# Retrieval and recurrent mixer of a two-layer hybrid trunk as one unrolled program on one Trainium2 core

## The chip, the core and the metric

The kernel runs on one core of a Trainium2 chip. The core has five engines, each with its own instruction stream: TensorE (PE; its weight loads are shown as PEld), VectorE (DVE), ScalarE (ACT), GpSimd (POOL) and SyncE (SP), and 16 DMA engines that carry data between HBM and the on-chip memory. Engines meet only at semaphores. The metric is the device time of one launch, in microseconds (us).

## What is computed

Two streams run through the same two layers: the **sample** (512 latent tokens, in four tiles of 128) and the **prompt** (128 context tokens, one tile). D_MODEL is 1024, everything is float32. Each layer is a mixer and then PEER, an expert retrieval. Layer 0's mixer is HGRN2 plus windowed attention, layer 1's is the RG-LRU block. The two streams share weights but no data: the sample reads cached context tensors that are inputs.

```python
for l in range(DEPTH):                       # DEPTH = 2
    h = _rmsnorm(x, norm1_g[l]) * (1 + sc1) + sh1
    y = _even_mixer(...) if l % 2 == 0 else _odd_mixer(...)
    x = x + g1 * y
    h = _rmsnorm(x, norm2_g[l]) * (1 + sc2) + sh2
    x = x + g2 * _peer(h, w_q[l], keys[l], u[l], v[l])
return _rmsnorm(x, final_g)

def blk(xb):                                 # _peer: 128 tokens, 8 heads, 16384 experts
    q = (xb @ w_q).reshape(128, 8, 2, 128)
    v1, i1 = top_k(q[:, :, 0] . keys[0], 16); v2, i2 = top_k(q[:, :, 1] . keys[1], 16)
    sc, pos = top_k(v1[:, None] + v2[None, :], 16)        # of the 16 x 16 sums
    eidx = take(i1 * 128 + i2, pos); g = softmax(sc)
    act = gelu(einsum('thkd,td->thk', u[eidx], xb))
    return einsum('thk,thkd->td', g * act, v[eidx])

def _odd_mixer(h, ...):                      # RG-LRU
    gate, xr = split(h @ w_in, 2)
    xc = conv(xr, width 4)
    r, i = sigmoid(xc @ w_a + b_a), sigmoid(xc @ w_x + b_x)     # 4 blocks of 256, two directions
    a = exp(-8 * softplus(-lam) * r); u = sqrt(1 - a*a) * (i * xc)
    h_t = a_t h_{t-1} + u_t                  # forwards and backwards
    return ((hf + hb) * gelu(gate)) @ w_out, last states
```

## The kernel before

`build` runs its parts one after another, each a `phase` with a barrier at its end: `modulation`, `even_mixer` (HGRN2 and attention), `project_and_peer` for layer 0, `rglru`, `project_and_peer` for layer 1.

**`project_and_peer`.** It first multiplies the mixer's output by `w_out` (`project`, L717, five tiles of 16 matmuls of 128x512), adds it to X (`residual`), norms (`norm`), turns the tiles for the query matmul (`turn`, L728) and makes the first unit's query (`first_query`), scores and route. `w_out`, the gain and shift rows live in the ring that the gathers use later, so POOL's third gather waits for the last projection and its seventh for the last norm. Then come 8 heads; in each head five **units**, one for each tile of 128 tokens (four of sample, then prompt). A unit takes the 16 best experts of every token, and so 16 **gathers**. One gather (L439, on POOL's queue) fetches, for each of the 128 tokens, one row `[u, v]` of 2048 floats: 1 MB. 8 heads x 5 units x 16 are 640 gathers a layer.

The way of one gather through the core: it lands in one of 10 ring slots (`SLOTS`); DVE multiplies its u half with the token's H and sums (`dot`, L658); ACT takes the gelu (L521); DVE makes a 128x128 diagonal of gate times gelu (`weight`, L666), after the next gather's dot; PE adds diagonal times v half into PSUM (L802, four matmuls, eight records in the trace); that frees the slot, on which POOL waits before it issues the gather ten places on. Between these, at fixed places of a unit, DVE routes the next unit in four pieces (`route_a` to `route_d`, at gathers 1, 3, 5 and 7), PE makes the next head's query (`query`, L753) and the next unit's scores, and ACT copies a finished unit's sum out of PSUM (`unpack`, L501), which DVE scales and adds to X (`add_unit`, L672 and L674). Heads 0 to 6 are one hardware loop (`Fori`) on every engine, head 7 is a copy of its body behind it. At the end of a head DVE does `add_unit` of the last tile, which waits for PE's last matmul and ACT's copy, before it goes back to the loop's start.

**`rglru`.** Four turns of a loop (RB = 4), each for 256 channels, all 640 tokens at once: PE projects (L1644), DVE convolves (L1588, L1593), PE makes the gates (L1659), ACT takes sigmoid, exp, tanh and sqrt (L1516 to L1535), DVE scans both ways (L1615) and writes the product to YT. No gather runs in it.

All engines work in the order in which their program is written; SP's queue carries the weights.

## Time and profile before

| | us |
|---|---|
| median of 3 runs (4525.49 to 4539.86) | 4538.74 |
| the profiled execution, whole | 4535.62 |
| its span in the trace | 4533.8 |
| first gather of layer 0 issued | 784.6 |
| last gather of layer 0 issued | 2451.7 |
| first gather of layer 1 issued | 2822.3 |
| last gather of layer 1 issued | 4495.5 |

The trace counts from the start of the span, and 1.8 us of the profiled execution lie outside it. The four gather times are starts of GpSimd's instructions at L439. The page gives each engine's busy time over the whole span; since the stages differ, the windows by stage are what to read: a line for each stretch, with busy time and number of instructions of every engine, TensorE's granted clock as a share of full speed, the busy share of the DMA engines (1.00 is all 16 busy all the time) and what they moved.

### The profile page before, as it was taken

The page shows a single profiled execution, that of the slowest core. Times are in us where ns is not written, and L with a number is a line of the kernel's source. Part 1 is how long each engine was busy: PE and PEld are TensorE (multiplying, and loading weights), DVE is VectorE, ACT ScalarE, POOL GpSimd, SP SyncE. Part 2 cuts the span into 40 slices and gives each one's busy share as a digit, 9 for nine tenths or more (in the row PEclk, how much of TensorE's full clock was granted, in tenths as well). Part 3 has the DMA queues.
Part 4 walks back from the last instruction along what each step waited for, and adds up shares of the span by engine and source line. Part 5 has one row for each costly group of instructions (what it writes and reads, how often), then busy time and mean ns, then how long its engine had stood idle before and what let it go on. Part 6 is the DMA issues. An engine that isn't in the chain of part 4 may idle for free. (4 is left out here: it accounts for less than half of the span.)

```text
span 4533.8 us, 54616 instructions
## 1 busy us (share of the span) xinstructions
PE 3131.9 (69%) x15503; PEld 1210.7 (27%) x15503; DVE 3204.4 (71%) x7667; ACT 1156.9 (26%) x2563; POOL 1468.5 (32%) x1316
## 2 busy tenths in 40 slices
PE   7698888766576766666655997767575666666655
PEld 2266564312121211112111553312121211112111
DVE  6633343778787878888887354778787878877886
ACT  4432141222222222221223341222222222221222
POOL 0000000344344444444443000344344444444443
PEclk9899968878786778778777998878686877787777
DMA  8510003999999999999997113999999999999998
GB/s 319 194 48 29 34 0 124 374 420 392 413 406 392 418 399 421 390 420 398 421 412 315 70 37 120 372 420 392 406 402 399 418 389 421 395 421 388 421 411 336
DMA packets 207051, 1468.87 MB, mean 324 GB/s; under 512 B 24281, under 2 KB 29161, under 8 KB 35689
## 3 DMA queue, kind: packets, MB, share of 16 engines
q0 software_dynamic: 184320, 1342.26, 72.2%
q1 hardware_dynamic: 21684, 121.29, 7.0%
q10 hardware_dynamic: 828, 2.76, 0.2%
q8 instruction: 94, 1.54, 0.1%
q14 instruction: 125, 1.02, 0.1%
HBM read 1462.84 MB, written 3.38 MB: 323 GB/s over the span
## 5 line engine op out<-in xcount | busy, mean ns | idle before, releaser
L802 PE MATMUL peer_acc<-peer_ring,peer_diag 64*64 64x512 f32 x10240 | 1749.6, 790 | 1125.9 <-DVE peer_diag L666 1122.1
L439 POOL DMA_INDIRECT peer_ring<-in_uv,peer_index x1280 | 1456.1, 1138 | 2494.4 <-PE peer_acc L802 1668.8
L658 DVE CUSTOM_DVE_ANT_0 peer_ring<-peer_ring,HY 128x1024 f32<-128x1024 f32 x1280 | 1561.8, 1221 | 398.7 <-DMA peer_ring<-in_uv,peer_index 311.1
L802 PEld LDWEIGHTS peer_acc<-peer_ring,peer_diag 64*64 64x64 f32 x10240 | 392.9, 160 | 2202.7 <-issue 2170.8
L521 ACT ACTIVATE peer_acts<-peer_dots 128x1 f32<-128x1 f32 x1280 | 258.6, 203 | 2498.6 <-DVE peer_dots L658 2497.9
L666 DVE TENSOR_SCALAR peer_diag<-ident,peer_acts,peer_gate 128x128 f32<-128x128 f32 x1280 | 439.1, 343 | 15.9 <-ACT peer_acts L521 14.5
L753 PE MATMUL peer_qp<-HT,peer_wq 128*128 128x512 f32 (+1 forms) x896 | 366.6, 539 | 0.0
L753 PEld LDWEIGHTS peer_qp<-HT,peer_wq 128*128 128x128 f32 x896 | 180.6, 224 | 373.8 <-issue 367.3
L501 ACT ACTIVATE peer_tmp<-peer_acc 64x512 f32<-64x512 f32 x320 | 189.0, 591 | 53.4 <-PE peer_acc L802 49.8
L672 DVE TENSOR_TENSOR peer_tmp<-peer_tmp,peer_G 128x1024 f32<-128x1024 f32 x80 | 98.0, 1225 | 89.9 <-ACT peer_tmp L501 83.4
L717 PE MATMUL peer_acc<-peer_ring,HY 128*128 128x512 f32 x320 | 144.6, 614 | 14.8 <-DMA peer_ring<-in_w_out 14.8
L1644 PE MATMUL lru_D<-HT,lru_wlru 128*128 128x128 f32 (+1 forms) x512 | 141.2, 438 | 14.2 <-DMA lru_wlru<-in_w_lru 11.6
L521 ACT ACT_TABLE_LOAD x100 | 128.3, 1283 | 1.8
L768 PE MATMUL peer_sc<-peer_keys,peer_qT 128*128 128x128 f32 x320 | 64.6, 327 | 61.4 <-issue 58.0
L658 DVE DVE_READ_ACCUMULATOR2_ANT peer_dots<- 128x1 f32 x1280 | 103.8, 81 | 0.0
L488 ACT ACT_TABLE_LOAD x80 | 102.6, 1283 | 1.9 <-ACT peer_qT L465 0.5
L251 DVE TENSOR_TENSOR mod_w_lo<-mod_wmod,mod_w_hi 128x4096 fp32r<-128x4096 f32 x16 | 70.8, 4425 | 44.0 <-DMA HY<-in_norm_g 16.5
L674 DVE TENSOR_TENSOR X<-X,peer_tmp 128x1024 f32<-128x1024 f32 x80 | 98.0, 1225 | 2.7
L1644 PEld LDWEIGHTS lru_D<-HT,lru_wlru 128*128 128x128 f32 x512 | 78.2, 192 | 77.4 <-issue 74.2
L961 POOL COPY hgrn_Vm<-hgrn_V 64x640 f32<-64x640 f32 x8 | 5.7, 715 | 281.4 <-ACT hgrn_V L991 281.2
L292 PE MATMUL mod_modp<-mod_w_hi,mod_cond_hi 128*2 128x512 f32 x192 | 77.3, 402 | 17.3 <-ACT mod_w_hi L223 17.1
L717 PEld LDWEIGHTS peer_acc<-peer_ring,HY 128*128 128x128 f32 x320 | 62.5, 197 | 92.8 <-issue 77.5
(281 smaller groups left out, 2973.1 us busy)
## 6 DMA issues: line engine op xcount, KB each, us to landing
mod_wmod<-in_w_mod SPq DMA_DIRECT2D x16, 2048.0 KB, 9.8
peer_ring<-in_uv,peer_index POOLq DMA_INDIRECT x1280, 16.3
HT<-in_w_mod SPq DMA_DIRECT2D x8, 2048.0 KB, 9.6
peer_wq<-in_w_q SPq DMA_DIRECT2D x16, 1024.0 KB, 11.7
peer_ring<-in_w_out SPq DMA_DIRECT2D x8, 1024.0 KB, 8.3
lru_wlru<-in_w_lru SPq DMA_DIRECT2D x4, 2048.0 KB, 8.4
hgrn_wqvg<-in_w_hgrn_qvg SPq DMA_DIRECT2D x4, 1536.0 KB, 6.7
peer_ring<-scratch_mod_rows SPq DMA_DIRECT2D x12, 512.0 KB, 13.7
```

Of the source, the lines that this page charges most:

```text
L439: pool.indirect_dma_start(ring[:, j % SLOTS, :], None, uv[:, :], bass.IndirectOffsetOnAxis(ap=index[:, j:j + 1], axis=0), element_offset=l ...
L488: act.activation(expo[:, :], top[:, :], ACT.Exp, bias=negtop[:, 0:1], accum_out=total[:, 0:1]).then_inc(exp_done, 1)
L501: last_copy = act.activation(tmp[r * HALF:(r + 1) * HALF, c * 512:(c + 1) * 512], acc[b % 2][c * HALF:(c + 1) * HALF, r * 512:(r + 1) * 51 ...
L521: act.activation(acts[:, j:j + 1], dots[:, j:j + 1], ACT.Gelu_apprx_tanh).then_inc(act_done, 1)
L658: dve.tensor_tensor_reduce(u, u, H[:, j // TOPK, :], 1.0, 0.0, ALU.mult, ALU.add, dots[:, j:j + 1]).then_inc(dot_done, 1)
L666: dve.tensor_scalar(diag[:, j % NDIAG, :], ident[:, :], acts[:, j:j + 1], gate[:, j:j + 1], ALU.mult, ALU.mult).then_inc(diag_done, 1)
L672: dve.tensor_tensor(tmp[:, :], tmp[:, :], G2[:, cond_of(b), :], ALU.mult).then_inc(tmp_done, 1)
L674: dve.tensor_tensor(X[:, b, :], X[:, b, :], tmp[:, :], ALU.add).then_inc(added, 1)
L717: last = pe.matmul(acc[b % 2][:, lo:lo + 512], H[:, b, k * P:(k + 1) * P], w_out[:, k, lo:lo + 512], start=(k == 0), stop=(k == KD - 1))
L753: last = pe.matmul(qp[:, lo:hi], wq[:, k, half * P:(half + 1) * P], HT[:, k, lo:hi], start=(k == 0), stop=(k == KD - 1), skip_group_check= ...
L802: last_mm = pe.matmul(acc[b % 2][c * HALF:(c + 1) * HALF, r * 512:(r + 1) * 512], diag[rows, j % NDIAG, rows], ring[rows, j % SLOTS, D + c ...
L1644: last = pe.matmul(Dp[2 * part + c][:, lo:hi], w[:, k, (part * W + c) * P:(part * W + c + 1) * P], HT[:, k, lo:hi], start=(k == 0), stop=( ...
```

## The change

`project_and_peer` and `rglru` are replaced by one phase, `trunk`, with no loop: every engine's program is written out over all 1280 gathers (g counts them), and `background()` generators put the other work at numbered gathers. The parts before it (`modulation`, `even_mixer`) are unchanged.

- **Order of units.** In a layer first the sample's 8 heads x 4 tiles (512 gathers), then the prompt's 8 heads (128). g 0 to 511 and 640 to 1151 are sample, 512 to 639 and 1152 to 1279 prompt. The prompt's heads all add up in PSUM, so it has one `unpack` and one add to X a layer, where it had eight.
- **Mixers beside gathers.** The sample's RG-LRU (512 tokens) stands at g 521 to 633, beside the prompt's gathers of layer 0. The prompt's (128 tokens) stands in heads 1 to 4 of the sample's gathers of layer 1 (g 738 to 957), its projection in head 5. Arrays of 512 or 128 tokens instead of 640 lie in ring slots.
- **Ring.** `ring_slots` gives each gather a slot: of 6 where w_out or the sample's mixer has the other four (g 0 to 63 and 512 to 703), of 9 where the prompt's mixer has one (g 704 to 1023), else of 10.
- **Diagonals.** For g 512 to 703 ACT makes them, in two instructions (L1316, L1320), not DVE.
- **Projections and norms.** Only tiles 0 and 1 and half of tile 2 are projected before the first accumulation of a layer (for layer 1, tile 0 beside the last gathers of layer 0); the others stand between the gathers. The prompt is projected at g 47 to 54 in layer 0, and in head 5 in layer 1.
- **Weights.** They come through two buffers of 1 MB (`wbuf`), 52 loads, on SP. RG-LRU's weights, w_out of layer 1 and the query weights of layer 1 are now read once for each stream; in all 60 MB of these weights where 36 were read (1 MB is 2^20 bytes here).
- **Small things.** POOL's and PE's waits are no longer followed by a `nop` and no longer compute a threshold in a register; the route of the next unit stands at gathers 4, 6, 8, 10 of a sample unit. The gain and shift of layer 1's first norm are applied by ACT as it copies the turned tile (8 instructions, `store_end`).

```diff
-        with nc.Block() as block: ... heads(pool, head) ... heads(act, head) ... heads(dve, head) ... heads(pe, head)
+RING = 10
+SMALL = 6
...
+def made_by_act(g):
+    return SAMPLE <= g < SPAN + SB * TOPK
...
+def ring_slots():
+    last, fills, table = {s: None for s in range(RING)}, [0] * RING, []
+    for g in range(SLOTS_IN_ALL):
+        if g < SB * TOPK or SAMPLE <= g < SPAN + SB * TOPK:
+            allowed = range(SMALL)
+        elif SPAN <= g < SPAN + 6 * SB * TOPK:
+            allowed = range(RING - 1)
+        else:
+            allowed = range(RING)
...
+            def _(pool):
+                for g in range(SLOTS_IN_ALL):
...
+                    if s == 0:
+                        pool.wait_ge(index_ready, u + 1)
+                    if g == INTERVAL:
+                        pool.wait_ge(projected, NB)
...
+                    if before is not None:
+                        pool.wait_ge(slot_free, before + 1)
+                    pool.indirect_dma_start(ring[:, slot, :], None, uv[:, :], ...
...
+                def weight(g):                                   # on ACT
+                    act.wait_ge(gate_ready, u + 1)
+                    act.wait_ge(act_done, g + 1)
+                    act.activation(prods[:, j:j + 1], acts[:, j:j + 1], ACT.Copy,
+                                   scale=gate[:, u % 2, g % TOPK:g % TOPK + 1]).then_inc(prod_done, 1)
+                    act.wait_ge(prod_done, diags_before(g) + 1)
+                    act.wait_ge(slot_free, g - NDIAG + 1)
+                    act.activation(diag[:, g % NDIAG, :], ident[:, :], ACT.Copy, scale=prods[:, j:j + 1]).then_inc(diag_a, 1)
...
+                    sample_lru = lru(lambda n, what: SAMPLE + 9 + 24 * n + {"xp": (9, 10), "gt": (18, 19), "sig": (22, 27),
+                                                                          "ex": (23, 32), "sq": (27, 36)}[what[0]][what[1]], 0)
...
+                    yield from lru(lambda n, what: SAMPLE + 9 + 24 * n + {"conv": (12, 13), "mix": (25, 34), "scan": (29, 38),
+                                                                         "y": (31, 40)}[what[0]][what[1]], 0)     # on DVE
+                    yield SPAN - 3
+                    residual(5, qp)
+                    yield SPAN - 1
+                    norm(5)
+                    r = route_a(HEADS * NB)
+                    route_b(r)
+                    route_c(r, HEADS * NB)
+                    route_d(r, HEADS * NB)
...
+                    yield from lru(lambda n, what: SAMPLE + 9 + 24 * n + {"xr": (0, 4), "gt": (8, 12), "rg": (16, 20)}[what[0]][what[1]], 0)
+                    yield SPAN - 1                               # on PE
+                    turn(5, acc[1])
...
+                    scores(HEADS * NB)
+                    pe.wait_ge(gated, 6)
+                    project(6, qp, range(0, KD), resident)
+                    pe.wait_ge(gated, 7)
+                    turn(6, qp)
```

Three places show how rows moved. The first is TensorE's stream where the sample's mixer begins; `lru_D<-HT,lru_wlru` before and `trunk_acc<-HT,trunk_wbuf` now are the same input projection. Before, in `rglru`, from the last input projection to the first gate:

```order
L1644 MATMUL lru_D<-HT,lru_wlru 128x512 x8
L1644 MATMUL lru_D<-HT,lru_wlru 128x128 x8
L1648 ISA
L1659 MATMUL lru_D<-lru_xc,lru_wrg 128x512 x2
L1659 MATMUL lru_D<-lru_xc,lru_wrg 128x128 x2
```

Now, at g 520 to 524 (the four matmuls of L2002 are one gather's accumulation):

```order
L1941 MATMUL trunk_qp<-ident,HY 128x128 x8
L2002 MATMUL trunk_acc<-trunk_ring,trunk_diag 64x512 x8
L2037 MATMUL trunk_acc<-HT,trunk_wbuf 128x512 x2
L2002 MATMUL trunk_acc<-trunk_ring,trunk_diag 64x512 x4
L2037 MATMUL trunk_acc<-HT,trunk_wbuf 128x512 x2
L2002 MATMUL trunk_acc<-trunk_ring,trunk_diag 64x512 x4
```

Two matmuls of 512 columns of the mixer now follow each gather's four, for 96 gathers in a row. The second place is ScalarE's stream in the same stretch; L1523 and L1374 are the gates' sigmoids. Before, in `rglru`:

```order
L1523 ACT_TABLE_LOAD
L1523 ACTIVATE lru_R<-lru_D,lru_par 128x640
L1522 REGISTER_ALU
L1523 ACTIVATE lru_I<-lru_D,lru_par 128x640
L1522 REGISTER_ALU
```

Now:

```order
L1374 ACT_TABLE_LOAD
L1374 ACTIVATE trunk_ring<-trunk_q,trunk_chan 128x512
L1374 ACTIVATE trunk_ring<-trunk_acc,trunk_chan 128x512 x2
L1374 ACTIVATE trunk_ring<-trunk_qp,trunk_chan 128x512
L1310 ACT_TABLE_LOAD
L1310 ACTIVATE trunk_acts<-trunk_dots 128x1
L1316 ACTIVATE trunk_prods<-trunk_acts,trunk_gate 128x1
L1320 ACTIVATE trunk_diag<-ident,trunk_prods 128x128
L1380 ACT_TABLE_LOAD
```

The gathers' gelu (L1310) stands between the mixer's functions, so each of them is followed by a reload; a turn of 24 gathers holds 13 of these loads, 72 small instructions for the gathers and 30 of 512 columns for the mixer. The third place is TensorE's stream where layer 1's retrieval begins. Before, its first rows after `rglru`:

```order
L717 MATMUL peer_acc<-peer_ring,HY 128x512 x32
L728 MATMUL peer_qp<-ident,HY 128x128 x8
L717 MATMUL peer_acc<-peer_ring,HY 128x512 x16
L740 MATMUL peer_q<-HT,peer_wq 128x128 x16
L768 MATMUL peer_sc<-peer_keys,peer_qT 128x128 x2
L717 MATMUL peer_acc<-peer_ring,HY 128x512 x32
```

Now, at g 639 and 640:

```order
L1928 MATMUL trunk_acc<-ident,HY 128x128 x8
L1954 MATMUL trunk_q<-HT,trunk_wbuf 128x128 x16
L1978 MATMUL trunk_sc<-trunk_keys,trunk_qS 128x128 x2
L1915 MATMUL trunk_qp<-trunk_ring,HY 128x512 x16
L1928 MATMUL trunk_qp<-ident,HY 128x128 x8
L1954 MATMUL trunk_q<-HT,trunk_wbuf 128x128 x16
L1915 MATMUL trunk_qp<-trunk_ring,HY 128x512 x8
L2002 MATMUL trunk_acc<-trunk_ring,trunk_diag 64x512 x4
```

The first tile's projection has gone ahead, among the last gathers of layer 0; one projection and a half, two turns and two queries stay between the last accumulation of layer 0 and the first of layer 1, where five projections stood.

## Rows read from the trace of the kernel before

**Rows 1.** The page's DMA queues: packets, MB, share of 16 engines.
```profile
q0 software_dynamic: 184320, 1342.26, 72.2%
...
q8 instruction: 94, 1.54, 0.1%
```

**Rows 2.** Busy windows by stage: us, busy (and count) by engine, clock, DMA, GB/s.
```profile
core 0: us, PE busy (x) PEld busy (x) DVE busy (x) ACT busy (x) POOL busy (x), PEclk, DMA share, GB/s
784.60:2451.70 1667.10, 1077.89 (x5837) 329.84 (x5839) 1340.29 (x3392) 384.62 (x1008) 724.02 (x640) 0.78 0.99 405
2451.70:2838.00 386.30, 314.66 (x1134) 168.08 (x1127) 174.84 (x286) 124.30 (x178) 12.11 (x17) 0.90 0.23 86
2838.00:4495.50 1657.50, 1071.54 (x5741) 317.85 (x5740) 1330.21 (x3381) 377.73 (x997) 719.30 (x629) 0.77 0.99 405
4495.50:4533.80 38.30, 17.77 (x80) 3.54 (x80) 20.09 (x36) 11.04 (x24) 0.99 (x1) 0.60 0.41 168
```

**Rows 3.** Windows again: a head's end, mid-head, whole head, head without loop.
```profile
1030.00:1040.00 10.00, 7.63 (x36) 2.19 (x36) 9.24 (x31) 3.19 (x8) 4.89 (x5) 0.73 0.87 324
...
1070.00:1220.00 150.00, 96.55 (x530) 26.70 (x533) 124.35 (x308) 33.71 (x91) 65.49 (x60) 0.82 1.01 421
...
1226.00:1437.00 211.00, 136.79 (x724) 41.44 (x724) 169.14 (x430) 47.28 (x126) 92.42 (x81) 0.77 1.00 409
...
2279.00:2450.00 171.00, 106.95 (x596) 27.35 (x596) 146.79 (x366) 49.09 (x122) 79.75 (x69) 0.76 1.01 415
```

**Rows 4.** The gathers' own line, L439: time from issue to landing.
```profile
DMA to landing us min/median/max: 5.4/16.3/22.7
```

**Rows 5.** VectorE's order of time at a head's end: start, us, what, [idle before].
```profile
1016.81 1.22 DVE L672 TENSOR_TENSOR peer_tmp<-peer_tmp,peer_G 128x1024 f32<-128x1024 f32 x1 [5.88 <-ACT peer_tmp L501]
...
1023.98 1.23 DVE L658 CUSTOM_DVE_ANT_0 peer_ring<-peer_ring,HY 128x1024 f32<-128x1024 f32 x1 [4.69 <-issue]
```

**Rows 6.** Groups by form between the gather stages: count, busy, mean ns, idle before.
```profile
L1644 PE MATMUL lru_D<-HT,lru_wlru 128*128 128x512 f32 x256 | 114.6, 601 | 14.2 <-DMA lru_wlru<-in_w_lru 11.6 <-ACT lru_I L1523 2.7
...
L1659 PE MATMUL lru_D<-lru_xc,lru_wrg 128*128 128x512 f32 x128 | 60.2, 593 | 0.0
...
L1615 DVE TENSOR_TENSOR_SCAN lru_HH<-lru_AA,lru_par,lru_I 128x512 f32<-128x512 f32 x16 | 20.5, 1284 | 0.6
...
L1603 DVE TENSOR_TENSOR lru_I<-lru_I,lru_xc 128x640 f32<-128x640 f32 x16 | 13.1, 818 | 0.0
...
L1523 ACT ACTIVATE lru_R<-lru_D,lru_par 128x640 f32<-128x640 f32 x16 | 12.7, 794 | 17.1 <-PE lru_D L1659 17.1
...
L1523 ACT ACT_TABLE_LOAD x4 | 5.1, 1283 | 0.1
```

**Rows 7.** Groups by form in one head, 1226 to 1437 us.
```profile
L658 DVE CUSTOM_DVE_ANT_0 peer_ring<-peer_ring,HY 128x1024 f32<-128x1024 f32 x80 | 97.6, 1221 | 24.6 <-DMA peer_ring<-in_uv,peer_index 17.8 <-issue 4.6 <-DVE peer_besti L587 1.1
...
L666 DVE TENSOR_SCALAR peer_diag<-ident,peer_acts,peer_gate 128x128 f32<-128x128 f32 x80 | 27.5, 343 | 0.1
...
L521 ACT ACTIVATE peer_acts<-peer_dots 128x1 f32<-128x1 f32 x80 | 16.2, 203 | 159.3 <-DVE peer_dots L658 159.3
```

**Rows 8.** TensorE's order of time at full clock: three gathers' accumulation.
```profile
2875.81 2.81 PE L802 MATMUL peer_acc<-peer_ring,peer_diag 64*64 64x512 f32 x24
```

**Rows 9.** VectorE's order of time before the first gather.
```profile
744.79 1.23 DVE L571 TENSOR_TENSOR HY<-HY,peer_ring 128x1024 f32<-128x1024 f32 x1
...
760.54 0.49 DVE L579 MAX8 peer_best<-peer_sc 128x8 f32<-128x128 f32 x2
...
765.29 0.42 DVE L606 FIND_INDEX8 peer_topi<-peer_top,peer_cand 128x8 uint32<-128x256 f32 x1
...
779.49 0.42 DVE L611 MAX8 peer_top<-peer_candw 128x8 f32<-128x256 f32 x1
...
783.39 0.18 DVE L629 TENSOR_TENSOR peer_index<-peer_pick 128x16 uint32<-128x16 f32 x1
```

**Rows 10.** The page's costliest groups: the output projections, five a layer.
```profile
L717 PE MATMUL peer_acc<-peer_ring,HY 128*128 128x512 f32 x320 | 144.6, 614 | 14.8 <-DMA peer_ring<-in_w_out 14.8
```

More of the change, by code:

```diff
@@ L1480, in body, with stream @@
+        def stream(b):
+            return (big, LS, 0) if b < SB else (small, LP, 1)
         with nc.Block() as block:
@@ L1631, in _ @@
+                weight(SLOTS_IN_ALL - 1)
+                add_sum(UNITS - 1)
+                end_norm(2 * NB - 1)
             @block.tensor
             def _(pe):
[L1634 to L1662 removed]
```

1747 lines of the change are left out of this document (1135 added, 612 removed).

## The prediction, made before the changed kernel was timed

> **What bounds the kernel now.** I read the windows by stage first, then windows inside the gather stages, then the groups by form. Layer 0's gathers are issued from 784.6 to 2451.7 us, layer 1's from 2822.3 to 4495.5 us. In both stages the DMA engines are 0.99 busy at 405 GB/s, while PE has 1077.9 and DVE 1340.3 of 1667.1 us [rows 2]. The gathers carry 1342 MB of the whole [rows 1]. So 83% of the span is set by the transfers: 640 gathers of 1.049 MB in 1667 us are 2.60 us each. Between the stages, in 386 us, DMA is 0.23 busy and PE works 314.7 us [rows 2]: mixer and projections, with no gather in flight. The span is 784.6 + 1667.1 + 370.6 (last issue of layer 0 to first of layer 1) + 1673.2 + 38.3 = 4533.8 us.
>
> Inside a stage there is a second loss. In mid-head windows the rate is 421 GB/s, over a whole looped head 409, and in the stretch just behind a loop's end 324 [rows 3]. At a head's end DVE waits 5.88 us for ACT's copy of the last unit and then stands 4.69 us with no releaser, at the loop's branch [rows 5]; no slot is freed meanwhile. The last head, which is followed by no branch, runs at 415 GB/s [rows 3].
>
> **The change part by part.** I build the new span from gather counts times a period for each stretch.
>
> *Start to first gather.* Before, DVE ended the norm of tile 1 at 746.0 us, and the route was cut in two and waited for later projections: its halves took 765.7 - 760.5 = 5.2 us and 783.6 - 779.5 = 4.1 us [rows 9]. Now the route follows norm 1 at once. Scores must be there; PE's second query waits for nothing that comes later, so I add 2 us. 746.0 + 2 + 9.3 is 757.3, and POOL issues at about 758 us, 27 us before the 784.6 of now. Bounds: 750 and 770.
>
> *g 64 to 511 (448 gathers, 10 slots).* Bytes: 448 x 1.049 MB, six loads of query weights, rows and keys, about 479 MB. Nothing loops, and `add_sum` no longer ends a head, so the stall of [rows 5] goes. I take 416 GB/s, between the 415 and 421 of [rows 3]: 1150 us. At the present 409 it is 1170.
>
> *g 512 to 639 (128 gathers, 6 slots, sample's mixer).* The mixer's turn n covers 24 gathers; costs of a turn on each engine:
> - PE: the 512-column matmuls of L1644 and L1659 took 114.6 and 60.2 us for four turns [rows 6], 43.7 a turn. Accumulating takes 2.81 us for three gathers at full clock [rows 8], 22.5 for 24. With 2 us of scores, 68 us, 2.84 a gather. I take full clock since PE then hardly pauses; while it did nothing but such work between the stages the granted clock was 0.90, against 0.78 beside gathers [rows 2].
> - DMA: 24 gathers and three loads of 1 MB, 28.3 MB, 67 us at 421 GB/s.
> - DVE: 169.1 us for 80 gathers [rows 3], less 0.34 for the diagonal [rows 7] and 0.15 for the adds, is 1.62 a gather, 39 us. The mixer adds 18 elementwise operations of 512 columns (818 ns for 640 columns [rows 6], some 0.66 us each) and 4 scans of 1.28 us, 17 us. 56 us.
> - ACT: 13 table loads at 1.28 us, 30 operations of 512 columns at 0.64 us (794 ns for 640 columns), 24 gelus and 24 products at 0.20 us [rows 6, 7], 24 diagonals. The trace shows no such diagonal; it lies between 0.20 us (one column) and 0.64 us (512), I take 0.3. 17 + 19 + 10 + 7 = 53 us, some 60 with the hops between them.
>
> All four lie between 56 and 68 us, and lumps of up to 6 us on ACT (load, four or six operations, load) hold up the diagonals. Six slots must cover them: a gather takes at least 5.4 us from issue to landing and typically 16.3 in the full queue [rows 4], which with 10 slots and 2.5 us a gather leaves 10 x 2.5 - 16.3 = 8.7 us for the work behind it. 8.7 + 5.4 = 14.1 us in six slots allows 2.35 us a gather, just under DMA's 2.5, so there is hardly any slack. I take 3.25 us for the 96 gathers beside the mixer and 2.75 for the other 32: 400 us. Bounds: 2.84 and 2.55 give 354 us; 4.0 and 3.0 give 480.
>
> *Hand-over to layer 1.* DVE's norm of tile 5 stands behind the last gather's dot. From the last issue: landing about 9 us, dot and norm 4, turn, store, query and scores 9, route 9.3, less one period: 29 us, 36 with seven hops of 1 us. Then PE makes one projection and a half before it accumulates; one is 144.6 / 10 = 14.5 us [rows 10], so with norm 6, turn and query the first slot comes free some 13 us after six slots would need it. Together 49 us, in place of 370.6. Bounds 35 and 75. Had this cover not been there, the four projections put among gathers would cost 58 us again.
>
> *g 0 to 63 and 640 to 703 (6 slots, projections and norms between the gathers).* In the first, DVE has 2.11 a gather (169.1 / 80) and 20 us of residuals and norms in 64, 2.43 us; I take 2.9, 186 us. In the second ACT makes the diagonals; 2.75, 176 us. Bounds for both: 2.55 and 3.3 us.
>
> *g 704 to 1279 (576 gathers, 9 or 10 slots).* 604 MB, 30 loads of 1 MB, keys and rows: 639 MB, 1536 us at 416 GB/s. The prompt's mixer adds 48 128-column matmuls a head to PE and about 10 us to DVE, which has 2.11 x 64 = 135 of 170 us; it is hidden. 8 us for jitter: 1544. At 409 GB/s, 1570. The 24 MB of repeated weight loads are in these bytes; by themselves they are 60 us.
>
> *End.* As now, 38 us from the last issue.
>
> *Sum.* 758 + 186 + 1150 + 400 + 49 + 176 + 1544 + 38 = 4301, and 2 us outside the span: 4303. The same account of before gave 4535.6 for the profiled execution, and the three runs have a median of 4538.7, so no correction; I say **4300 us**, 5.3% less. Of the 235 us, 322 come from the gap and 27 from the start. Within the stages 116 go back: their bytes rise from 1353 MB (405 GB/s x 3340 us) to about 1404, 122 us at 416 GB/s, the six slots and jitter cost 81 more, and the loop ends give 88.
>
> *A rule against it.* The gather stages move 405 GB/s over 1667 us and 421 in mid-head [rows 2, 3]. The Trainium skill, page "DMA: Bandwidth & Descriptors", section "Specifications", gives an HBM limit per core of about 358 GB/s; by that figure the 1118 MB of the two long stretches would take 3120 us, not 2690. The rows decide: this trace is above it already.
>
> **The rivals.**
> 1. *Lockstep beside the mixer.* Six slots, diagonals from an ACT with 60 of 68 us full, and a PE without slack: each waits for the other's lump. Price: 4.0 us and 3.0 us a gather in g 512 to 639 (+80), 3.3 in the other two six-slot stretches (+57): 4440. For it: the slack above of 0.15 us a gather. Against: the steps leave two or more gathers between producer and consumer.
> 2. *The loop ends were not the loss.* Then 409 GB/s or less stays; at the stages' mean of 405, which includes them, the long stretches take 1118 / 0.405 = 2760 us, 70 more, and I allow as much again for the late index of a sample unit (gather 8, where it was 5): 4370 to 4440. Against: [rows 3], 415 where no branch follows.
> 3. *Everything overlaps.* The bounds from below: 354 us beside the mixer, 2.55 in the six-slot stretches (-36), hand-over 35: 4205.
> 4. *Slower: the unrolled program starves for instructions.* Fetches go by the DMA engines, that are now never idle: one queue shows 94 packets, 1.54 MB [rows 1], 16 KB each. At a loop's branch an engine stood 4.69 us [rows 5]. If 60 such fetches, out of a number that was 94 with loops and can only be of that order without, each stood exposed for 4.69 us in turn, they would add 280 us: 4580, slower than now. It decides from about 50 exposed fetches. Against: within a head, straight code of hundreds of instructions an engine runs at 421 GB/s [rows 3].
>
> On rival 4, the Trainium skill, page "Runtime: NRT & Kernel Launch", section "Instruction fetch mechanics", says that sequential fetch is mostly hidden and that a taken branch out of the window stalls. The 4.69 us at the branch agrees with the second half; by the first half rival 4 costs nothing.
>
> That the change does not do what it says is excluded for the order: mixer matmuls do stand between accumulations.
>
> **How the numbers follow.** Forecast 0.60 (4240 to 4360), rival 1 0.15, rival 2 0.10, rival 3 0.11, rival 4 0.04. The range 4205 to 4420 takes in the forecast, rival 3's price and the lower half of rivals 1 and 2, which leaves out under 2 in 10. Faster by more than 0.3% (about what a measurement of this kernel can tell from no change) is all but rival 4: 0.95; within it 0.01; slower 0.04.
>
> **What would show it.** Windows of the new trace: first gather near 758 us; g 64 to 511 at 415 GB/s or more with no dip every 210 us (else rival 2); the span from g 512 to 639 near 400 us, PE's clock above 0.9 and PE busy over 85% (if PE waits for ACT's diagonals and DMA falls under 0.8, rival 1); 40 to 55 us between the issues of g 639 and 640; stretches of idle "issue" time on PE or DVE in straight code would be rival 4. The forecast is wrong if DMA is not the last to be waited for in g 64 to 511 and 704 to 1279.

## The result and the profile after

The changed kernel takes **4379.2 us** (median of 4 runs, 4376.5 to 4382.0); the kernel before took 4536.6 us on the same chip. The ratio is 0.9657, 95% interval 0.9639 to 0.9675: 3.4% less. The forecast was 4300 us, the range 4205 to 4420. So sign and range held, and 79 us of the expected gain did not come. The profiled execution has a span of 4376.7 us; the forecast's sum without its 2 us outside the span was 4301.

The same stretches as in the prediction, from the issue times of the gathers (a stretch runs to the issue of the next gather):

| stretch | forecast us | measured us | difference |
|---|---|---|---|
| start to first gather | 758 | 751.7 | -6 |
| g 0 to 63, six slots | 186 | 202.9 | +17 |
| g 64 to 511, ten slots | 1150 | 1161.5 | +11 |
| g 512 to 639, six slots, sample's mixer | 400 | 428.5 | +29 |
| hand-over, issue 639 to 640 | 49 | 35.2 | -14 |
| g 640 to 703, six slots | 176 | 208.2 | +32 |
| g 704 to 1279 | 1544 | 1552.7 | +9 |
| end | 38 | 35.9 | -2 |

In the span the differences add up to 76 us. The three stretches with six slots make 78 of them, and the others nearly cancel. The page of after, its DMA part, to be set beside [rows 1]:

```profile
DMA packets 227797, 1494.28 MB, mean 341 GB/s; under 512 B 25016, under 2 KB 48360, under 8 KB 55400
...
q0 software_dynamic: 184320, 1342.26, 75.4%
q1 hardware_dynamic: 35364, 133.37, 8.0%
...
q8 instruction: 111, 1.82, 0.2%
```

The gathers' bytes are the same. Instruction fetches on q8 rose from 94 to 111 packets, not by a multiple (the other queue for instructions went from 125 to 118). Now the windows by stage, in the order of the table (columns: window, us, then busy us and count of PE, PEld, DVE, ACT, POOL, then PE's clock, DMA share, GB/s); they answer to [rows 2, 3]. The third holds the 96 gathers 521 to 616 beside the sample's mixer, the fourth gathers 617 to 639, the fifth the hand-over, the seventh heads 1 to 4 of layer 1 beside the prompt's mixer.

```profile
751.70:954.60 202.90, 151.68 (x696) 48.46 (x695) 144.15 (x349) 45.45 (x112) 74.34 (x65) 0.85 0.87 334
954.60:2116.10 1161.50, 776.24 (x4137) 200.11 (x4135) 942.75 (x2418) 263.94 (x721) 539.54 (x448) 0.81 1.01 414
2144.60:2465.90 321.30, 287.69 (x1161) 88.41 (x1162) 230.51 (x499) 206.63 (x455) 114.27 (x97) 0.95 0.93 355
2465.90:2544.70 78.80, 53.25 (x225) 15.51 (x224) 47.15 (x80) 53.28 (x114) 24.75 (x23) 0.83 0.95 379
2544.70:2579.90 35.20, 28.25 (x122) 14.24 (x121) 16.47 (x47) 9.80 (x20) 1.60 (x1) 0.81 0.13 50
2579.90:2788.10 208.20, 152.96 (x728) 53.95 (x730) 130.37 (x291) 97.68 (x252) 69.57 (x65) 0.82 0.86 334
2788.10:3499.50 711.40, 460.25 (x2604) 148.96 (x2596) 558.19 (x1479) 233.97 (x561) 295.35 (x256) 0.84 0.99 404
```

The stretch with ten slots is close to the forecast: DMA full at 414 GB/s (416 forecast) over 1161 us, with no loop end in it. The gap of 370.6 us is 35.2. But three rows have a DMA share of 0.86 to 0.93 and 334 to 355 GB/s. What waits there, beside the mixer (2144.6 to 2465.9; us in total, times, longest):

```profile
PE trunk_acc L2002 <- ACT trunk_diag L1320: 32.8, 17, 5.1
...
DVE trunk_ring L1689 <- DMA trunk_ring<-in_uv,trunk_index: 48.6, 29, 4.3
DVE trunk_best L1622 <- PE trunk_sc L1978: 26.2, 6, 6.0
...
POOL trunk_ring L1224 <- PE trunk_acc L2002: 205.4, 96, 7.1
```

PE (L2002, the accumulation) waits 32.8 us for ACT's diagonals and works nearly all the rest. POOL waits before every gather for PE's freeing of a slot. DVE stands 26.2 us before a route, since PE has not made the scores yet.

From the traces I also took, for every gather, its **round**: the times between its issue, the start and end of its dot, the end of its gelu, start and end of its diagonal, first and last of its matmuls, and the next issue into the same slot. The sum divided by the number of slots is the period. Means in us:

| kernel, gathers (slots) | issue to dot | dot | to gelu's end | to diagonal | diagonal | to matmul | matmuls | to next issue | round |
|---|---|---|---|---|---|---|---|---|---|
| after, 64 to 511 (10) | 19.85 | 1.22 | 0.28 | 2.27 | 0.34 | 0.16 | 1.42 | 0.44 | 25.99 |
| after, 0 to 63 (6) | 11.41 | 1.22 | 0.79 | 2.49 | 0.34 | 1.40 | 1.30 | 0.59 | 19.54 |
| after, 521 to 616 (6) | 10.99 | 1.22 | 1.95 | 0.42 | 0.40 | 3.35 | 1.11 | 0.37 | 19.83 |
| after, 640 to 703 (6) | 11.81 | 1.22 | 2.14 | 0.42 | 0.40 | 2.00 | 1.34 | 0.56 | 19.89 |
| of these, 646 to 703 (6) | 11.36 | 1.22 | 1.44 | 0.43 | 0.40 | 1.52 | 1.36 | 0.58 | 18.31 |

The last row leaves out the first six gathers of layer 1, whose slots are all free and whose accumulations stand behind PE's projections: their round is 35.1 us. The seventh is issued 31.0 us after the first; the 58 behind that take 177.2 us, 3.06 each. POOL's longest wait of this stretch is in it:

```profile
POOL trunk_ring L1224 <- PE trunk_acc L2002: 135.9, 55, 22.9
```

How much a stretch varies by itself: in four profiled executions in which nothing was changed beside the sample's mixer, its 96 gathers took 316.7, 321.3, 322.4 and 322.8 us. A difference of some 6 us in one stretch is therefore not shown by one execution.

### The profile page after: what moved, and what is told of

It reads as the page before. It is cut to its first block, busy times and chain, and to the rows that moved or that the text cites. A ratio compares the mean times of both kernels' runs of the same rounds, so it can differ in the third digit from the quotient of the medians.

```text
span 4376.7 us, 47845 instructions
## 1 busy us (share of the span) xinstructions
PE 3113.1 (71%) x15504; PEld 1108.5 (25%) x15504; DVE 3098.1 (71%) x7502; ACT 1371.1 (31%) x3138; POOL 1516.1 (35%) x1310
## 2 busy tenths in 40 slices
DMA packets 227797, 1494.28 MB, mean 341 GB/s; under 512 B 25016, under 2 KB 48360, under 8 KB 55400
## 3 DMA queue, kind: packets, MB, share of 16 engines
q1 hardware_dynamic: 35364, 133.37, 8.0%
## 4 chain that ended last, share of the span: by engine, by line
DMA 31%; DVE 20%; PE 16%; issue 10%; ACT 4%; POOL 1%; DVEq 0%; ACTq 0%; POOLq 0%
DMA trunk_ring<-in_uv,trunk_index 28%; PE trunk_acc L2002 8%; DVE trunk_ring L1689 5%; DMA trunk_wbuf<-in_w_lru 2%; DVE trunk_diag L1698 2%; PE trunk_qp L1915 2%; POOL trunk_ring L1224 1%; PE trunk_q L1954 1%; PE trunk_q L2037 1%; DVE trunk_onehot L1664 1%; DVE trunk_onehot L1660 1%; DVE trunk_pick L1667 1%; DVE trunk_work L1625 1%; DVE trunk_besti L1637 1%; ACT L1310 1%
## 5 line engine op out<-in xcount | busy, mean ns | idle before, releaser
L2002 PE MATMUL trunk_acc<-trunk_ring,trunk_diag 64*64 64x512 f32 x10240 | 1712.5, 763 | 1031.6 <-DVE trunk_diag L1698 922.6
L1224 POOL DMA_INDIRECT trunk_ring<-in_uv,trunk_index x1280 | 1504.1, 1175 | 2336.0 <-PE trunk_acc L2002 1948.9
L1689 DVE CUSTOM_DVE_ANT_0 trunk_ring<-trunk_ring,HY 128x1024 f32<-128x1024 f32 x1280 | 1560.5, 1222 | 567.5 <-DMA trunk_ring<-in_uv,trunk_index 544.5
L1310 ACT ACTIVATE trunk_acts<-trunk_dots 128x1 f32<-128x1 f32 x1280 | 257.0, 202 | 2260.4 <-DVE trunk_dots L1689 2255.7
L2002 PEld LDWEIGHTS trunk_acc<-trunk_ring,trunk_diag 64*64 64x64 f32 x10240 | 331.3, 154 | 2233.9 <-DVE trunk_diag L1698 1834.6
L1698 DVE TENSOR_SCALAR trunk_diag<-ident,trunk_acts,trunk_gate 128x128 f32<-128x128 f32 x1088 | 373.7, 343 | 101.8 <-ACT trunk_acts L1310 101.8
L1961 PE MATMUL trunk_qp<-HT,trunk_wbuf 128*128 128x512 f32 x448 | 276.9, 703 | 0.0
L1310 ACT ACT_TABLE_LOAD x139 | 178.3, 1283 | 2.5
L1303 ACT ACTIVATE trunk_tmp<-trunk_acc 64x512 f32<-64x512 f32 x264 | 155.5, 589 | 5.0 <-PE trunk_acc L2002 2.1
L1915 PE MATMUL trunk_qp<-trunk_ring,HY 128*128 128x512 f32 x224 | 111.8, 633 | 9.0 <-DMA trunk_ring<-in_w_out 9.0
L2037 PE MATMUL trunk_q<-HT,trunk_wbuf 128*128 128x128 f32 (+1 forms) x304 | 64.5, 370 | 60.6 <-DMA trunk_wbuf<-in_w_lru 60.6
L1954 PE MATMUL trunk_q<-HT,trunk_wbuf 128*128 128x128 f32 x768 | 105.1, 298 | 3.4 <-ACT HT L1265 2.2
L1294 ACT ACT_TABLE_LOAD x80 | 102.6, 1283 | 1.4
## 6 DMA issues: line engine op xcount, KB each, us to landing
trunk_wbuf<-in_w_lru SPq DMA_DIRECT2D x16, 1024.0 KB, 22.6
```

Of the source, the lines that this page charges most:

```text
L1224: pool.indirect_dma_start(ring[:, slot, :], None, uv[:, :], bass.IndirectOffsetOnAxis(ap=index[:, u % 2, s:s + 1], axis=0), element_offset ...
L1294: act.activation(expo[:, :], top[:, :], ACT.Exp, bias=negtop[:, 0:1], accum_out=total[:, 0:1]).then_inc(exp_done, 1)
L1303: last = act.activation(tmp[r * HALF:(r + 1) * HALF, c * 512:(c + 1) * 512], acc[acc_of(u)][c * HALF:(c + 1) * HALF, r * 512:(r + 1) * 512 ...
L1310: act.activation(acts[:, j:j + 1], dots[:, j:j + 1], ACT.Gelu_apprx_tanh).then_inc(act_done, 1)
L1689: dve.tensor_tensor_reduce(u_rows, u_rows, HY[:, b, :], 1.0, 0.0, ALU.mult, ALU.add, dots[:, j:j + 1]).then_inc(dot_done, 1)
L1698: dve.tensor_scalar(diag[:, g % NDIAG, :], ident[:, :], acts[:, j:j + 1], gate[:, u % 2, g % TOPK:g % TOPK + 1], ALU.mult, ALU.mult).then_ ...
```

## The experiments

Theory at the start: beside the mixer PE's own work is the limit and six slots give it no slack. Rivals: ACT's lumps (lockstep), late weights in short packets, and the slots themselves.

**1. Weights laid out contiguously.** The pieces `xr` and `gt` of the mixer are column halves of one array, so each partition's 8 KB come in eight runs of 1 KB. On the page of after the row for them shows a median of 22.6 us to landing against 9.4 for the query weights:

```profile
trunk_wbuf<-in_w_q SPq DMA_DIRECT2D x24, 1024.0 KB, 9.4
...
trunk_wbuf<-in_w_lru SPq DMA_DIRECT2D x16, 1024.0 KB, 22.6
```

```diff
-                    cols = slice(0, 2 * P) if kind == "xr" else slice(2 * P, 4 * P)
-                    return io["w_lru"][i, :, :].rearrange("p (k n) -> p k n", k=KD)[:, :, cols]
+                    return io["w_lru"][i, kind == "gt", :, :]      # stored as two halves
```

> The changed kernel with w_in's pieces of the recurrent mixer laid out so that each partition's 8 KB are contiguous in HBM (before: eight runs of 1 KB, which is where 19,000 more packets under 2 KB come from). Theory A, the short packets delay the weights and take DMA time from the gathers: PE's wait for the buffer of in_w_lru falls from 60.6 us over the run to under 15, the gathers beside the prompt's mixer (heads 1 to 4 of layer 1) go from 2.77 to about 2.69 us each, the 96 beside the sample's mixer from 3.35 to 3.2; together 20 to 35 us less, about 4350 us. Theory B, the stretches beside the mixer are set by PE and ACT and the late weights are only a symptom: under 8 us of change, 4371 to 4387.

Measured: 4362.2 us (4359.8 to 4370.4), ratio to before 0.9633 [0.9617, 0.9649], 17 us less. The page's packets under 2 KB fell from 48360 to 31976, and the landing of the same megabyte to 9.9 us:

```profile
trunk_wbuf<-in_w_lru SPq DMA_DIRECT2D x16, 1024.0 KB, 9.9
```

PE's 60.6 us of waiting for these buffers in the changed kernel, all in the prompt's mixer, no longer appear:

```profile
PE trunk_q L2037 <- DMA trunk_wbuf<-in_w_lru: 60.6, 4, 15.8
```

The stretch of g 704 to 959 went from 711.4 to 689.1 us (2.78 to 2.69 a gather), at this window:

```profile
2781.60:3470.70 689.10, 457.62 (x2600) 143.47 (x2592) 559.90 (x1476) 232.52 (x557) 311.35 (x257) 0.87 1.01 415
```

Theory A is right for the prompt's mixer (with 8 us given back in the next 96 gathers). For the sample's nothing is shown: its 96 gathers took 318.5 us, 3 less, which is within what the stretch varies by.

**2. The kernel before, its head loop written out.** Nothing else is changed.

```diff
-            with eng.Fori(0, HEADS - 1) as h:
+            for h in range(HEADS - 1):
                 body_of_head(h, False)
```

> The kernel before, in which only the hardware loop over seven heads is written out in straight code on every engine of the retrieval; the order of the work is unchanged. By the prediction's term the loop ends cost some 88 us of before over both layers, of which the wait of 5.88 us for ACT's copy stays in this kernel: 14 loop ends by about 4.7 us are 66 us, so 4470 us, ratio 0.985, and no window behind a head's end at 324 GB/s. By rival 2, the loop ends were covered by transfers in flight: ratio 0.997 to 1.003. By rival 4, straight code starves for instructions: slower than before.

Measured: 4477.4 us (4474.6 to 4483.5), ratio 0.9882 [0.9866, 0.9899]: 54 us less. The two gather stages took 1643.2 and 1648.3 us where they took 1667.1 and 1673.2:

```profile
780.10:2423.30 1643.20, 1069.53 (x5827) 325.83 (x5829) 1337.83 (x3392) 376.40 (x1002) 720.12 (x640) 0.79 1.00 411
```

That is 49 us for 14 loop ends, 3.5 us each, less than the 4.69 us of idle time in [rows 5]. That the gathers in flight cover the rest is likely, but not shown. VectorE's order of time at the end of a head shows what is gone and what stays: the wait for ACT's copy before the sum, and then the next head's dot with no idle time:

```profile
1009.01 1.23 DVE L672 TENSOR_TENSOR peer_tmp<-peer_tmp,peer_G 128x1024 f32<-128x1024 f32 x1 [3.99 <-ACT peer_tmp L501]
...
1011.41 1.22 DVE L658 CUSTOM_DVE_ANT_0 peer_ring<-peer_ring,HY 128x1024 f32<-128x1024 f32 x1
```

Rivals 2 and 4 of the prediction both fall here: the loop ends were a loss, and straight code costs less than the loop did. What its own fetches cost is not measured apart from that. A third of the whole gain of 157 us could have been had by this alone.

**3. Less PE work, less ACT work, both.** All three shorten only the sample's mixer. The first leaves out three of the eight k-steps of its projections. The second uses gelu for sigmoid, exp, tanh and sqrt, so that most of ACT's table changes go. Not all of them, as its expectation has it: in the 96 gathers 14 of 46 table loads stay, mostly for the routes' exp (L1294) and the gelu behind it.

```diff
+                                    if which == 0 and KD // 2 <= k < KD - 1:
+                                        continue                                        # PE
...
-                                act.activation(buf["R"][c][d], buf["R"][c][d], ACT.Sqrt)
+                                act.activation(buf["R"][c][d], buf["R"][c][d], ACT.Gelu_apprx_tanh if which == 0 else ACT.Sqrt)
```

> The changed kernel, in which three of the eight k-steps are left out of every projection matmul group of the sample's mixer (12 of 32 matmuls of 512 columns a turn, some 10.7 of 44 us by the trace of before); all waits, loads and ACT and DVE work stay. If PE is the limit beside the sample's mixer (90% busy there, clock 0.95), the 96 gathers go from 3.35 us to about 2.9 each, some 43 us less in all. If PE is only in step with ACT's diagonals and lumps, they stay at 3.2 or more and the whole changes by under 15 us.

> The changed kernel, in which sigmoid, exp, tanh and sqrt of the sample's mixer are all replaced by gelu, so that ACT never changes its table beside it; same number and sizes of instructions. It takes 13 table loads of 1.28 us, 17 us, out of the 53 us or more that ACT works in a turn. If ACT's lumps are what PE waits for (lockstep), the 96 gathers go from 3.35 to about 3.0 us each and PE's wait of 32.8 us for ACT's diagonals goes: 30 us less in all. If PE's own work is the limit, 3.25 us each and 10 us less.

> The changed kernel with both cuts of the first series at once in the sample's mixer: three of eight k-steps left out of its projections, and gelu in place of sigmoid, exp, tanh and sqrt. One by one they shortened the 96 gathers from 321.3 to 312.7 and to 304.4 us, far less than the 43 us and 17 us a turn of engine time that they take out. Theory coupling: PE's own work and its waits for ACT's diagonals trade for each other, so that the two together give more than their sum of 25.5 us: under 290 us, on the way to the 2.74 us a gather, 263 us, that six slots allowed with nothing beside them. Theory third limit (slots and DMA at 3.1 us a gather): about 296 us, the sum, or more.

Measured for g 521 to 616 (whole kernel in brackets): 312.7 us (4370.8, ratio 0.9646 [0.9630, 0.9662]), 304.4 us (4361.5, 0.9631 [0.9615, 0.9647]), and together 294.3 us (4352.9, 0.9612 [0.9596, 0.9629]). Windows of the three kernels, in this order:

```profile
2145.20:2457.90 312.70, 255.71 (x1065) 75.00 (x1066) 229.87 (x499) 207.13 (x457) 111.68 (x96) 0.89 0.94 364
```

```profile
2141.10:2445.50 304.40, 281.00 (x1162) 87.19 (x1163) 228.95 (x498) 163.82 (x424) 115.08 (x97) 0.97 0.97 377
```

```profile
2146.40:2440.70 294.30, 245.90 (x1065) 71.59 (x1066) 229.86 (x499) 163.47 (x423) 116.66 (x96) 0.94 0.98 387
```

The gelu's reloads, in the changed kernel and in the second:

```profile
L1310 ACT ACT_TABLE_LOAD x21 | 26.9, 1283 | 0.4
```

```profile
L1310 ACT ACT_TABLE_LOAD x6 | 7.7, 1283 | 0.1
```

Taking 32 us of work from PE bought 8.6 us, little more than the stretch varies by; the whole kernel's ratio overlaps that of the changed kernel. PE's wait for ACT's diagonals rose by 22 us from the 32.8 of after (waits of PE in that window, first kernel):

```profile
PE trunk_acc L2002 <- ACT trunk_diag L1320: 54.8, 26, 6.4
```

Taking 43 us from ACT bought 17, and the two together 27, about their sum and clear of the noise. So neither theory alone was right, and the coupling that I expected to see released did not show; the 296 us of the third limit came. PE at 90% is not the limit by itself: with 18% of PE's time idle the stretch is nearly as long. ACT's table loads are worth more than PE's matmuls, and with both cuts the DMA engines are 0.98 busy at 387 GB/s, so that little more can come.

**4. The slots.** Five slots for the sample's mixer, and six for every gather of the kernel.

```diff
+        if SAMPLE <= g < SPAN:
+            allowed = range(SMALL - 1)          # five slots; the other kernel: range(SMALL) for all g
```

> The changed kernel with five slots in place of six for g 512 to 639, nothing else. Theory slots: the 19.8 us of a slot's round stay, or shrink by at most 1.5 us because fewer transfers are in flight: 3.67 to 3.97 us a gather, the 96 gathers beside the sample's mixer take 352 to 381 us where they took 321. Theory PE (90% busy there): the matmuls set the pace and the slots only follow, 321 us plus at most 8.

> The changed kernel with six ring slots for every gather, not only where projections or the sample's mixer use the other four. It tells what six slots cost when nothing stands beside the gathers. Theory slots: a slot's round (issue, 11 us to the start of the dot, some 8 us of dot, gelu, diagonal and matmul, next issue) sets the time; with 6.1 us behind the start of the dot, as in g 64 to 511 of the changed kernel, and 11.2 us before it, the round is 17.3 us, 2.88 a gather in g 64 to 511 (1161 to 1290 us) and a little more in layer 1, 4650 us in all. By the prediction's account (8.7 us behind, 5.4 us to land, 2.35 us a gather) six slots just suffice: 2.6 a gather, under 4400 us.

Measured: with five slots the 96 gathers took 328.7 us (one run, 4393.0 us in all), 7 more, far from the 352 us or more of the theory of slots. With six everywhere, g 64 to 511 took 1227.6 us, 2.74 a gather against 2.59, and the whole 4535.0 us (one run), as much as the kernel before. The windows, five slots first, then g 64 to 511 of the kernel with six everywhere:

```profile
2149.50:2478.20 328.70, 293.88 (x1165) 90.61 (x1166) 226.83 (x495) 207.05 (x455) 115.05 (x97) 0.94 0.91 343
```

```profile
958.50:2186.10 1227.60, 818.95 (x4170) 204.78 (x4173) 951.84 (x2432) 268.77 (x732) 506.02 (x448) 0.78 0.98 392
```

| kernel, gathers (slots) | issue to dot | dot | to gelu's end | to diagonal | diagonal | to matmul | matmuls | to next issue | round |
|---|---|---|---|---|---|---|---|---|---|
| six everywhere, 64 to 511 (6) | 10.09 | 1.22 | 0.30 | 2.39 | 0.34 | 0.19 | 1.49 | 0.42 | 16.45 |
| five slots, 521 to 616 (5) | 9.41 | 1.22 | 1.61 | 0.42 | 0.40 | 2.50 | 1.14 | 0.36 | 17.06 |
| both cuts of 3, 521 to 616 (6) | 11.69 | 1.22 | 0.94 | 0.42 | 0.40 | 1.87 | 1.12 | 0.46 | 18.12 |

The time from issue to landing in the stretch g 64 to 511 (shortest, median, longest), with ten slots in after and with six in the other:

```profile
DMA to landing us min/median/max: 14.6/18.9/27.6
```

```profile
DMA to landing us min/median/max: 5.9/8.9/16.7
```

Beside the mixer the round shrinks with the slots (19.83 to 17.06): less time in the queue before the dot, and less waiting between diagonal and matmul. There the slots follow the engines, and the theory of slots is refuted for that stretch. With only queries, scores and routes beside the gathers, six slots cost 0.15 us a gather, not the 0.29 that I expected, and not the nothing of the prediction's account. DVE makes the diagonals in that stretch, 2.39 us behind the gelu, and the DMA engines are 0.98 busy in it.

**5. Fewer bytes.** The 20 loads that the change repeats for the prompt carry 512 of 2048 columns, so the prompt's mixer and most of its queries are computed from other weights.

```diff
+                    if name[0] == "qp" or (name[0] in ("xr", "gt", "rg") and name[2]):
+                        sp.dma_start(wbuf[i % 2][:, 0:D // 2], w_q[0, :, 0:D // 2]).then_inc(piece_in[i % 2], 16)
+                        return
```

> The changed kernel, in which the 20 loads that the change repeats for the prompt (12 pieces of its mixer's weights, 8 of query weights) carry only 512 of 2048 columns, 0.26 MB in place of 1.05: 15.7 MB fewer in layer 1, and its short packets mostly gone too. Theory bytes: 15.7 MB at 416 GB/s are 38 us, and 22 us came from the layout already (first series), of which most is in this too: g 704 to 1279 goes from 1553 to 1495 to 1515, about 4325 to 4340 us. If the gathers there wait for slots or engines and not for bandwidth: no more than the 17 us of the layout, 4360.

Measured: 4330.7 us (4329.7 to 4331.6), ratio 0.9555 [0.9539, 0.9570]; g 704 to 1279 took 1504.1 us where after took 1552.7 and the contiguous layout 1538.0. Queue q1 moved 117.64 MB in place of 133.37. The 34 us below the layout's time stand for 15.7 MB, 38 us at 416 GB/s: in that stretch time goes by bytes.

**6. Route later; makers of the diagonals.** Both with the contiguous layout.

```diff
-    return (2, 4, 6, 8, 10) if u % (HEADS * NB) < SB else (0, 1, 3, 5, 7)
+    if u % (HEADS * NB) < SB:
+        return (2, 4, 6, 8, 10)
+    return (0, 3, 5, 7, 9) if SAMPLE <= u * TOPK < SPAN + SB * TOPK else (0, 1, 3, 5, 7)
```

> The changed kernel with the contiguous layout of the mixer's weights (4362 us in the first series), and with the route's steps of g 512 to 703 at 0, 3, 5, 7, 9 in place of 0, 1, 3, 5, 7, so that DVE does not stand behind PE's scores (26 us in g 521 to 616, 18 in 640 to 703), a wait in which it holds up the dots behind it. If that wait lengthens the slots' round: 3.35 to 3.2 us a gather beside the mixer and as much in g 640 to 703, 15 to 25 us less than with the layout alone, 4340. If it only fills time in which the next gather has not landed: within 5 us of 4362.

Measured: 4358.0 us (4354.1 to 4359.3), ratio 0.9611 [0.9595, 0.9627], within 5 us of the 4362 with the layout alone, as the second theory has it: no gain of the later route is clear of the noise. The 96 gathers took 313.9 us in place of 318.5, those of g 640 to 703 210.3 in place of 210.4. DVE's wait for the scores went from 26.2 to 1.3 us and mostly came back as other waits (waits of DVE, g 521 to 616; these lines number one less than in after):

```profile
DVE trunk_ring L1688 <- DMA trunk_ring<-in_uv,trunk_index: 58.1, 34, 4.9
DVE trunk_ring L1773 <- ACT trunk_ring L1384: 15.7, 5, 4.2
...
DVE trunk_best L1621 <- PE trunk_sc L1977: 1.3, 1, 1.3
```

> The kernel with the contiguous layout and the later route, with the makers of the diagonals changed in the two stretches of six slots that have projections among the gathers: ACT makes those of g 0 to 63 (DVE before), DVE those of g 640 to 703 (ACT before). In g 0 to 63 a diagonal by DVE begins 2.49 us after its gelu, since it stands behind the next gather's dot; by ACT it would be 0.42. If this lengthens the slots' round of 19.5 us and the round sets the time, the stretch falls from 203 to some 183 us. In g 640 to 703 ACT's gelus end 2.14 us after the dot where DVE makes the diagonals in 0.79; the swap takes 1.35 us out of the front and puts 2.07 back: 210 to 215 us. If PE's projections set the pace (PE busy 152 of 203 us), neither changes by over 4 us.

Measured: 4348.0 us (4347.0 to 4351.7), ratio 0.9602 [0.9585, 0.9619]. g 0 to 63 fell from 203.2 to 189.0 us, 14 less of the 20 expected; g 640 to 703 rose from 210.3 to 216.0. In the first, the round went from 19.54 to 18.39: a diagonal by ACT starts 0.42 us after its gelu, by DVE 2.49. The gelus then end later (1.32 for 0.79) and PE takes them up later (1.85 for 1.40), so that 1.15 of the 2.07 us come through. The round is the pace there, and its middle part counts.

**7. The three edits together.** Contiguous layout, later route, and ACT's diagonals in g 0 to 63 beside those that it makes already.

```diff
-    return SAMPLE <= g < SPAN + SB * TOPK
+    return g < SB * TOPK or SAMPLE <= g < SPAN + SB * TOPK
```

> The changed kernel with the three edits that gained: contiguous layout of the mixer's weights, the route's later steps in g 512 to 703, and diagonals by ACT in g 0 to 63 as well as in g 512 to 703. If the pieces add up: layout and route gave 4358, ACT's diagonals in the first 64 took 14 us off that stretch, and DVE's in g 640 to 703 had cost 6: 4342 to 4346 us, some 35 us below the changed kernel. If the engines give it back in the stretch behind, 4358.

> The changed kernel as it is, on the same chip and in the same rounds as the kernel with all three edits: 4376 to 4382 us as before if the difference of the two is to be trusted, ratio 0.966.

Measured side by side: 4341.0 us (4338.7 to 4342.3), ratio to before 0.9581 [0.9568, 0.9595]; the changed kernel 4379.8 us (4370.4 to 4383.9), 0.9663 [0.9648, 0.9678]. The three edits are worth 39 us, 0.9% of the changed kernel; 4341.0 is just under the 4342 to 4346 us expected if the pieces add up. The layout and the diagonals are clear pieces of it, the later route is not. The first stretch, beside the first row of the windows above:

```profile
751.10:940.20 189.10, 144.18 (x693) 47.02 (x691) 127.90 (x289) 86.50 (x232) 73.93 (x65) 0.88 0.91 358
```

## Why the prediction held, and where it was off

The measured 4379 us lies in the stated range, but outside the band of 4240 to 4360 us that was given 0.60, and inside the 4370 to 4440 of rival 2, whose mechanism experiment 2 refutes. So the range held, while the most likely band did not. Of the signs named beforehand, PE's clock (0.95), its busy share (90%) and DMA above 0.8 came beside the mixer; g 64 to 511 ran at 414 GB/s and not 415, and the 35.2 us between the issues of g 639 and 640 lie under the 40 to 55.

**The bound and the long stretches: right.** 1150 us were forecast for g 64 to 511 and 1544 for g 704 to 1279; 1161.5 and 1552.7 came, at 414 GB/s in the first. Experiment 5 shows that the second goes by bytes. Its excess of 9 us has a cause that the prediction had not looked for: the 1 KB runs of the mixer's pieces, 15 us over the stretch in experiment 1. "Hidden" was right of the prompt's mixer's matmuls and wrong of its loads. PE waited 60.6 us for four of them and its accumulations stood behind.

**Loop ends: the mechanism right, the size shown in part.** 88 us were given to the loop ends with the sum behind them, the worth of 416 GB/s in place of 405. Experiment 2 took 54 us out, 49 of them in the gather stages. It leaves the wait for ACT's copy in place, so the rest of the 88 is not shown.

**Start and hand-over: right.** 751.7 for 758. For the hand-over, 35.2 us, not 49. The sum's first part (29 us by durations, 36 with hops) was the whole of it. The 13 us for a first slot that comes free late are real, but lie in the next stretch: its seventh gather is issued 31.0 us after the first, and six gathers at the 3.06 us of the later ones would be 18.3. That is 12.7 us. The table above therefore shows 13 us too little for the hand-over and 13 too much for g 640 to 703: together they were forecast at 225 us and took 243.

**Six slots with projections among the gathers: the step that failed.** This is the term for g 0 to 63 (2.9 us forecast, 3.17 measured) and g 640 to 703 (2.75 forecast, 3.06 measured behind the late start), 17 and 19 us. The prediction took 5.4 us from [rows 4], the shortest landing, and 8.7 us for all work behind it, and found 14.1 us in six slots, 2.35 a gather. The runs show the other split. With six slots and only queries, scores and routes beside them, the dot begins 10.1 us after the issue and 6.4 us follow: 16.45 us, 2.74 a gather. So the 2.75 taken for g 640 to 703 was all that six slots took with DVE's diagonals and no projection or norm beside them. The 58 gathers from g 646 on have a round of 18.31 us, 1.9 more. PE comes later to the diagonal (1.52 us for 0.19), with projections in its queue; ACT ends its gelus later (1.44 for 0.30), with norms, copies and the diagonals in its own; the dot begins 1.3 us later; and 2.0 us come back, since ACT's diagonal begins 0.43 us behind the gelu where DVE's began 2.39. When DVE made the diagonals (experiment 6) the gelus ended 0.77 us behind the dot, so over half of ACT's delay goes with its diagonals. What six slots allow with ACT's diagonals and nothing else beside them no run shows. Experiment 6 shows for g 0 to 63 that a shorter middle part shortens the stretch.

**Beside the sample's mixer: nearly right, for reasons half right.** 3.25 us a gather were forecast, 3.35 measured. The 3.25 was a choice between PE's 2.84 and the 4.0 of lockstep, and no sum gave it, so that it came near is in part luck. PE: 68 us a turn were forecast, 287.7 / 4 = 72 came. The forecast took full clock, the granted clock was 0.95, and 68 us at that clock would be some 72 (an estimate, 68 / 0.95). The accumulations were busy 110.1 / 96 = 1.15 us each against 0.94 from [rows 8], and the mixer's records were longer than on their own (L2037 636 to 650 ns in the mean, where [rows 6] has 601). Part of that is overlap: the busy times of PE's groups add up to 301 us in a stretch in which PE is busy 287.7. In the order of time a gather's accumulation and its two mixer matmuls follow each other every 2.93 us, where the forecast's terms make 2.76. The lines that show it:

```profile
L2002 PE MATMUL trunk_acc<-trunk_ring,trunk_diag 64*64 64x512 f32 x768 | 110.1, 646 | 32.8 <-ACT trunk_diag L1320 32.8
L2037 PE MATMUL trunk_qp<-HT,trunk_wbuf 128*128 128x512 f32 x112 | 58.7, 648 | 0.0
```

```profile
2174.40 1.09 PE L2002 MATMUL trunk_acc<-trunk_ring,trunk_diag 64*64 64x512 f32 x8
2175.41 1.98 PE L2037 MATMUL trunk_acc<-HT,trunk_wbuf 128*128 128x512 f32 x4
2177.33 1.09 PE L2002 MATMUL trunk_acc<-trunk_ring,trunk_diag 64*64 64x512 f32 x8
```

The diagonal took 0.40 us (0.3 taken), the product 0.30 (0.20). All four engines' sums (72, DMA full for some 75 of 80, 58 and 52 us) lie below the 80 us that a turn took. The mechanism is the one that I had as rival 1, at a fraction of its price: in experiment 3, 32 table loads fewer on ACT are worth 17 us and 32 us less of PE's work 9, and by experiment 4 the slots are not what decides. **The 32 gathers around it** were taken at 2.75, again with nothing for the work beside them; they took 107 us for 88. In g 617 to 639, PE waited 15.4 us for diagonals of ACT, which has mixer and norm to do, and 9.0 us for rows of `w_out` that can be loaded only when the last scans have left the slots:

```profile
PE trunk_acc L2002 <- ACT trunk_diag L1320: 15.4, 4, 6.2
PE trunk_qp L1915 <- DMA trunk_ring<-in_w_out: 9.0, 1, 9.0
```

No experiment was made on these, so how much of the 19 us each is worth stays open.

**The rivals.** Rival 1 is there in part: its 80 us for g 512 to 639 came as 29, of which 10 are beside the mixer. Its price for the other two stretches, 3.3 us a gather (60 us over the forecast; the 57 of the prediction is a slip), was nearly reached in what was measured there, 49 us, but 13 of these are the late first slot. Rival 2 and rival 4 are refuted by experiment 2, rival 4 also by the trace: PE's only wait in g 64 to 511 is for diagonals, and none is without a releaser. Rival 3 needed 2.55 us a gather with six slots; the shortest that any run shows for them is 2.74. **The rule against it** bore out no better than before: the stretches with ten slots moved 414 to 416 GB/s, above the 358 GB/s that the Trainium skill, page "DMA: Bandwidth & Descriptors", section "Specifications", gives for a core; the measurement decides. It was taken with one core running, and no run here shows what a busy neighbour would change. The kernel with its loop written out ran 1.2% faster (experiment 2). The Trainium skill, page "Runtime: NRT & Kernel Launch", section "Instruction fetch mechanics", says that sequential fetch is mostly hidden; by that rule straight code costs nothing, and the gain is in keeping with it, though 54 us came where 66 were expected and nothing was measured apart.

One reading of the prediction is wrong, and no term of its sum rests on it: the two gather stages are 3340 of 4534 us, 74% of the span and not 83%.

## What to carry to other kernels

When a ring is made smaller, don't take the shortest landing for the round: take the whole round from issue to next issue, stretch by stretch, and add what stands in each engine's queue ahead of the gather's own steps; the bare floor is no forecast for a stretch with other work in it. Where several engines are each 64 to 93% busy in one stretch, expect each cut to bring a fraction of itself, and price cuts by trying them. When a shared load is split in two, look at the shape of the pieces: column halves of a weight array landed in 22.6 us where contiguous ones took 9.9.

## What the runs showed of the hardware

- The landing of a 1 MB gather follows the number in flight: median 18.9 us (shortest 14.6) with ten slots, 8.9 us (shortest 5.9) with six, at 414 and 392 GB/s. Four slots of ten bought 22 GB/s.
- The same megabyte of weights, beside the gathers, landed in 22.6 us in 1 KB runs and in 9.9 us in 8 KB runs.
- A loop's branch that left DVE idle for 4.69 us [rows 5] cost the gather stages 3.5 us each time (49 us for 14).
- The records of matmuls of 512 columns lasted 636 to 650 ns in the mean between accumulations of 64x64 tiles at a clock of 0.95, and 601 ns in the stretch of before at 0.90 where nothing stood between them; records overlap, so this is not the time that each costs.
- ACT's table load took 1283 ns. At 2555.23 us of the changed kernel one began 0.02 us behind the instruction before it and the next instruction 0.01 us behind the load, so that a change of table cost 1.3 us there.
